# Two layers of the second block: token blocks of the output projection in another order, and four probability copies moved ahead of exponentials

## The reference, cut to what matters

```python
def hybrid_layer(x, ...):
    h = rmsnorm(x, norm_w)
    aq, ak, av, ag, bq, bk, bv, bg, cu, cg = split(h @ w_in)        # 1024 -> 4608
    o_a = diff_attention(aq, ak, av, ...) * silu(ag)    # 4 heads, two softmax maps m = 0, 1 of width 64
    o_b = retention(bq, bk, bv, ...)      * silu(bg)    # 4 heads
    o_c = multiscale_pool(cu, ...)        * silu(cg)    # 4 groups
    return x + concat([o_a, o_b, o_c]) @ w_out          # 1536 -> 1024
```

## Time and profile before

| | |
|---|---|
| median of 3 runs | 2766.0 us (2764.51 to 2766.5) |
| the profiled execution | 2769.01 us, span 2767.2 us, mean granted TensorE clock 0.992 |
| TensorE busy | 2710.3 us (98% of the span) |
| VectorE busy | 1857.4 us (67%) |
| ScalarE busy | 1323.2 us (48%) |
| GpSimd busy | 140.4 us (5%) |
| chain that ended last | PE 84%, DVE 8%, ACT 4%, DMA 1%, the rest about 1% each or less |

### The profile page before, as it was taken

One profiled execution on the slowest core, in us unless ns is written; L12 is line 12 of the kernel. 1 busy time (PEld: TensorE's weight loads), 2 busy tenths in 40 slices (PEclk: granted clock), 3 DMA queues, 4 the chain that ended last, 5 costly groups with the idle time before them and its releaser, 6 DMA issues.

```text
span 2767.2 us, 44384 instructions
## 1 busy us (share of the span) xinstructions
PE 2710.3 (98%) x17512; PEld 1740.6 (63%) x17512; DVE 1857.4 (67%) x2793; ACT 1323.2 (48%) x2116; POOL 140.4 (5%) x119
## 2 busy tenths in 40 slices
PE   9999999999999999999999999999999999999999
PEld 6886476654688646885566654688546555465544
DVE  7994475646899539993576555999446775567754
ACT  4663365543566425662465442566333535335442
POOL 1000022100100001000022000100000002000010
PEclk9999999999999999999999999999999999999999
DMA  5443312222344332433322212444332231322312
GB/s 162 112 118 114 122 49 67 84 77 84 92 111 117 118 116 79 118 105 118 107 69 62 84 61 99 122 115 113 114 122 92 64 104 61 107 73 68 93 61 84
DMA packets 325306, 265.66 MB, mean 96 GB/s; under 512 B 25228, under 2 KB 288652, under 8 KB 324528
## 3 DMA queue, kind: packets, MB, share of 16 engines
q1 hardware_dynamic: 322608, 254.57, 29.8%
q10 hardware_dynamic: 1952, 7.05, 1.0%
q0 software_dynamic: 608, 2.11, 0.2%
HBM read 257.40 MB, written 4.21 MB: 95 GB/s over the span
## 4 chain that ended last, share of the span: by engine, by line
PE 84%; DVE 8%; ACT 4%; DMA 1%; DVEq 1%; issue 1%; SPq 0%; ACTq 0%; POOL 0%
PE pu L471 12%; PE pu L472 12%; PE pu L473 12%; PE pu L598 6%; PE pu L597 6%; PE pu L599 6%; PE pm L471 5%; PE pm L472 5%; PE pm L473 5%; PE pm L597 2%; PE pm L598 2%; PE pm L599 2%; PE pm L896 2%; DVE w_lo L1089 2%; PE pm L669 2%; PE pm L883 1%
## 5 line engine op out<-in xcount | busy, mean ns | idle before, releaser
L1089 DVE SCALAR_TENSOR_TENSOR w_lo<-stage,w_hi 128x2048 f16<-128x2048 f32 (+1 forms) x156 | 356.8, 2287 | 399.0 <-ACT w_hi L1818 394.8
L1818 ACT ACTIVATE w_hi<-stage 128x2048 f16<-128x2048 f32 (+1 forms) x147 | 273.3, 1859 | 498.2 <-PE pm L473 376.2
L471 PE MATMUL pu<-h_hi,w_hi 128*128 128x512 f16 x912 | 348.3, 382 | 5.9 <-DVE w_lo L1089 5.9
L472 PE MATMUL pu<-h_lo,w_hi 128*128 128x512 f16 x912 | 347.6, 381 | 0.0
L473 PE MATMUL pu<-h_hi,w_lo 128*128 128x512 f16 x912 | 347.3, 381 | 0.0
L471 PE MATMUL pu<-w_hi,arena 128*128 128x512 f16 x512 | 196.2, 383 | 6.5 <-ACT arena L2131 6.5
L472 PE MATMUL pu<-w_lo,arena 128*128 128x512 f16 x512 | 196.3, 383 | 0.0
L473 PE MATMUL pu<-w_hi,arena 128*128 128x512 f16 x512 | 195.9, 383 | 0.0
L471 PE MATMUL pm<-w_hi,arena 128*128 128x512 f16 x512 | 194.0, 379 | 0.0
L472 PE MATMUL pm<-w_lo,arena 128*128 128x512 f16 x512 | 194.0, 379 | 0.0
L473 PE MATMUL pm<-w_hi,arena 128*128 128x512 f16 x512 | 194.0, 379 | 0.0
(11 more groups left out here) (330 smaller groups left out, 6225.4 us busy)
## 6 DMA issues: line engine op xcount, KB each, us to landing
stage<-in_w_in_dram SPq DMA_DIRECT2D x136, 512.0 KB, 4.5
stage<-in_w_ffn_gate_dram SPq DMA_DIRECT2D x88, 512.0 KB, 3.9
stage<-in_w_ffn_up_dram SPq DMA_DIRECT2D x88, 512.0 KB, 5.1
stage<-in_w_ffn_down_dram SPq DMA_DIRECT2D x80, 512.0 KB, 4.0
stage<-in_w_out_dram SPq DMA_DIRECT2D x40, 512.0 KB, 4.2
stage<-in_w_in_dram SPq DMA_DIRECT2D x24, 256.0 KB, 3.3
stage<-in_w_ffn_down_dram SPq DMA_DIRECT2D x16, 256.0 KB, 4.2
stage<-in_w_branch_hgrn_dram SPq DMA_DIRECT2D x8, 512.0 KB, 3.5
```

Of the source, the lines that this page charges most:

```text
L471: nc.tensor.matmul(ps, w1, r_hi, start=first, stop=False)
L472: nc.tensor.matmul(ps, w1, r_lo, start=False, stop=False)
L1089: V.scalar_tensor_tensor(out=w_lo[:, s, 0:n], in0=stage[:, s, 0:n], scalar=WSCALE, in1=w_hi[:, s, 0:n], op0=ALU.mult, op1=ALU.subtract).th ...
L1818: A.activation(w_hi[:, s, 0:n], stage[:, s, 0:n], ACT.Copy, scale=WSCALE).then_inc(hi_split, 1)
```

## The change: what it does

In the tensor engine's list: (a) `scores2` has its waits ahead of the one matmul whose bank they guard, rather than ahead of both; in slots 8 and 12 map 1 goes first. (b) The first pass of the output projection takes token blocks 0 and 1 through all four chunks, after the Silus up to ("cg", 0), and then blocks 2 and 3, after the last Silu. In ScalarE's list: (c) in slots 8 and 12 the copy of the transposed probabilities stands ahead of the exponentials; before and elsewhere it stands behind them. In VectorE's list: (d) the retention heads and pool groups wait for the Silu of the values that they use, not for the last one owed.

```diff
@@ tensor: scores2
-                if i >= 2:
-                    pe.wait_ge(pt_ready, t.at("pt_ready", i - 1))
-                if i % 4 == 2 and i > 2:
-                    pe.wait_ge(o_sq, t.now("o_sq"))
-                if i in (8, 12):
-                    pe.wait_ge(o_cp, t.next("o_cp"))
-                if i % 4 == 3 and i > 3:
-                    pe.wait_ge(o_rt, t.next("o_rt"))
                 hd, b = divmod(i, NB)
-                for m in range(2):
+                for m in (1, 0) if i in (8, 12) else (0, 1):
+                    if m == 0 and i >= 2:
+                        pe.wait_ge(pt_ready, t.at("pt_ready", i - 1))
+                    if m == 1 and i % 4 == 2 and i > 2:
+                        pe.wait_ge(o_sq, t.now("o_sq"))
+                    if m == 1 and i in (8, 12):
+                        pe.wait_ge(o_cp, t.next("o_cp"))
+                    if m == 1 and i % 4 == 3 and i > 3:
+                        pe.wait_ge(o_rt, t.next("o_rt"))
@@ tensor: mixer2, first pass of the output projection
-                        pe.wait_ge(evac_a, t.now("evac_a"))
-                    for n, (at, k) in enumerate(slot_ks[i % 3]):
...
+                        for unit in range(2):
+                            pe.wait_ge(evac_a, t.now("evac_a") - 1 + unit)
+                            for n, (at, k) in enumerate(slot_ks[0]):
+                                pe.wait_ge(m_ready, t.now("m_ready") + n + 1)
+                                for b in (2 * unit, 2 * unit + 1):
+                                    last = token_part(pu[b], b, 0, [(at, k)], acc, k == 0, False)
@@ vector: mixer2_slot, retention heads
-                    settle()
+                    v.wait_ge(evac_a, t.at("evac_a", evacuated(MIX2_ORDER.index(("bg", (hd - 1) // 2)) + 1, True, MIX2_ORDER)))
@@ vector: pool_post
-                    settle()
+                    v.wait_ge(evac_a, t.at("evac_a", evacuated(MIX2_ORDER.index(("cg", gr // 2)) + 1, True, MIX2_ORDER)))
@@ vector: mixer2, after pool_post()
+                settle()
@@ scalar: mixer2_slot; taken(i) is the wait for pt_done and the copy to AT that stood in the slot
+                if q in (8, 12):
+                    taken(q - 1)
                 if q < 16:
                     ...   (wait for mx_ready, two exponentials)
...
-                if 1 <= q <= 16:
...
+                if 1 <= q <= 16 and q not in (8, 12):
+                    taken(q - 1)
```

More of the change, by code:

```diff
@@ L1007, in mixer2 @@
                         pe.wait_ge(evac, t.now("evac") + 2)
-                        pe.wait_ge(evac_a, t.now("evac_a"))
-                    for n, (at, k) in enumerate(slot_ks[i % 3]):
[L1010 to L1013, removed]
+                        for unit in range(2):
[4 more added lines that the diff above has]
+                                    last = token_part(pu[b], b, 0, [(at, k)], acc, k == 0, False)
+                    else:
+                        for n, (at, k) in enumerate(slot_ks[i % 3]):
+                            if i < 3:
+                                pe.wait_ge(m_ready, t.now("m_ready") + 4 * i + n + 1)
+                            for b in range(NB):
+                                last = token_part((pu if i < 3 else pm)[b], b, i % 2, [(at, k)], acc, k == 0, k == OUT2_LATE[-1])
                     last.then_inc(unit_done, 1)
@@ L2085, in copy_scale, with taken @@
                 A.activation(r_post[:], ps[:], ACT.Copy).then_inc(o_cp, 1)
+            def taken(i):
+                s_.wait_ge(pt_done, t.next("pt_done"))
+                b = i % NB
+                A.activation(AT[:, :, b * P:(b + 1) * P], pm[2 * (i % 2)][:].rearrange("p (k c) -> p k c", k=NB), ACT.Copy).then_inc(pt_ready, 1)
             def mixer2_slot(q):
```

## The result

The changed kernel takes 2745.34 us (median of 4 runs, 2744.75 to 2745.9), the kernel before 2766.25 (4 runs). The ratio is 0.9925, with a 95% interval of 0.9913 to 0.9938: 20.9 us less. In a later comparison it was 2743.88 (5 runs) against 2766.51 (9 runs), ratio 0.9923 (0.9909 to 0.9936).

A forecast was written before the change was run, and what follows sets the result against it. The prediction took TensorE, busy for 98% of the span, as the bound. Its terms, 7.4 + 6.7 + 7.4 + 0 = 21.5 us off the 2766.0 median, gave 2744.5 us, with a range of 2740 to 2752.

The forecast's parts named there:

- (c), 7.4 us: Scores of slots 9 and 13, both layers: moving the probability copy up removes four stalls, 3 x 1.78 + 2.05 us.
- next meeting point: Scores of slot 10, where TensorE next needs ScalarE's copies: ScalarE is in time, so none of the gain is given back.
- slack that was put at 0.38 us: Before slot 10's scores: ScalarE's copies end at 2195.29, the scores want to start at 2195.67, leaving 0.38 us.
- (b), 6.7 us: Output projection's start, once per layer: splitting the first pass removes the whole 3.35 us stall for the last Silu.
- The clock, 7.4 us: TensorE's slow clock behind stalls: 1.64 us in slot 9, 2.58 and 3.15 in first projection passes, all taken as won.
- The rival in which it doesn't come back: Projection: the clock falls anyway at the pool products, so only 14.1 us are gained, 2752; chance 0.10.
- (a), 0: Score pairs of slots 7, 11 and 15: moving the wait gains 0 us, as the later matmul still waits.
- the wait isn't won back: Rival at scores of slots 7, 11 and 15: moving the wait gains another 2.3 us, 2742; chance 0.08.
- no pair comes apart: Rivals denied: score pairs come apart where a wait stands between (2761 us, chance 0.03) or in every slot (2778, 0.02).
- (d), 0: VectorE's last retention head starts some 4 us earlier, but half a projection pass hides it anyway: 0 us.
- More falls in the timed runs: Rival at slots 9 and 13: all four stalls lose 1.64 us, not one, so 4.9 more gained, 2739.6; chance 0.07.

The follow-up runs named there:

- only_b: Kernel before the change with only the output projection's first pass split into two halves: 2755.06 us, ratio 0.9958.
- no_d: Changed kernel without VectorE's waits for the Silu of the values it uses: 2745.69 us, ratio 0.9929 to the kernel before.
- filler: Kernel before the change with 28 spare matmuls in TensorE's wait at the start of the output projection, the wait kept: 2761.91 us, ratio 0.9985.
- one_half: Changed kernel with both score matmuls of a pair on the same rows of the array: 2770.64 us, ratio 1.0019 to the kernel before.
- only_a: Kernel before the change with only the score waits moved next to the matmul they guard: 2764.88 us, ratio 0.9998.
- only_c: Kernel before the change with only the probability copy moved ahead of the exponentials in slots 8 and 12: 2757.3 us, ratio 0.9969.
- before: The kernel without any of the changes: 2766.25 us, median of 4 runs.
- only_d: Kernel before the change with only VectorE waiting for the Silu of the values it uses: 2764.99 us, ratio 0.9995.
- pool_late: Changed kernel with slot 28's last pool product behind the first half of the projection's first pass: 2742.37 us, ratio 0.9915 to the kernel before; again 2742.64.

## Why the prediction was right, step by step

- **(c), 7.4 us:** 7.4 measured, with the next meeting point as worked out. The slack that was put at 0.38 us is 0.21. ScalarE came up a little less than worked out: its high half starts 7.96 us after the scores of slot 8 (8.40 before, so 0.44 instead of 0.49), and its squares 15.21 after them, where the working gives 15.04. The step holds, with less to spare than it said.
- **(b), 6.7 us:** 6.9. The lone score matmul with its 1.05 us was the nearest row, but the pool product is followed after 0.96. Half a pass hides the last Silu (`only_b`), also without (d) (`no_d`).
- **The clock, 7.4 us:** 6.8. The fall in slot 9 was right at 1.6. The first passes were over-counted by 0.26 us each: I compared them with 10.36, the distance between two high halves, but from the first product to the first high half it's 10.62 at full clock. That the clock is lowered by the standing still, assumed in the prediction, is shown by `filler` and `only_b`. The rival in which it doesn't come back is out.
- **(a), 0:** 0.6. The reason was right, `one_half` shows the pair's concurrency by itself. The size was a little off: the successor comes 1.42 us after the first of the two, 0.10 a place sooner than the wait and the pair one after the other. (By starts the wait costs 0.46 us, 8.05 less 7.59, where the view lists 0.39 of idle time.) The rivals are out: the wait isn't won back, and no pair comes apart.
- **(d), 0:** 0.3 beside the other parts, by the tails of `no_d` and the changed kernel, and not told from none in the medians. The reason given holds for the projection, where half a pass hides VectorE's head. What it missed lies elsewhere: a low weight half that came late, and VectorE's pause in slot 7 of the second layer.
- **More falls in the timed runs:** the prediction called the four stalls of part (c) alike and put the one fall down to the phase. They weren't alike: the one with the fall was the longest, 2.05 us against 1.78 by its own figures, and the same one shows it in all four profiles that have VectorE's pause as well as the stall. The other three show none in any profile. The projection's two starts show a fall in all four kernels that keep the stall without a filler (`before`, `only_a`, `only_c`, `only_d`). There the stall is 3.27 us each time, but the first passes take from 11.95 to 13.51 us, so what the slow clock costs does vary. The Trainium skill ("TensorE: Matmul & The Clock Gate", "Part 1: The HAM clock gate") says that the point at which the clock changes depends on the phase in which the work meets the gate; these differing lengths agree with it.

The errors (+0.2, -0.6, +0.6) nearly cancelled, so 2744.5 against 2745.34 is closer than the terms. Some of that is luck. The terms come from one profile with a mean clock of 0.992, while the timed runs of the same kernel beside the experiments had 0.994 to 0.996. In four profiles the two first passes together took 5.2, 4.0, 3.0 and 5.3 us more than twice 10.62, 4.4 on average. By that an average run would gain 0.8 us less than this profile: an estimate, which would account for most of the way from the tail's 22.0 us to the medians' 20.9.

What stays open: why VectorE pauses without (d), and whether the length of a stall alone decides over the fall of the clock.

## What to carry to other kernels

When one engine is busy nearly all the time, list its few waits, and for each ask three things: what the waiting instruction was queued behind, which engine is late at the next meeting point once the wait is gone, and whether the clock fell after it. Here the slow clock behind the stalls was a third of the gain, and spare matmuls alone won most of that third without removing a stall. Moving a wait from a pair of concurrent matmuls to one of them wins next to nothing, since the pair ends with its later member.

## What the runs showed that I had not expected

The same instructions ahead of the change take different times. The first score pair of the second block starts at 2119.6, 2118.1 and 2115.8 us in the profiles of the kernel before and two of the changed one, and as early as 2115.3 in `only_c`; the program of the first block is the same in all. Much of this is slow clock in some executions and not in others. From 484 to 499 us the granted clock is 0.89 in the two late ones and 1.00 in the two early ones, and the late ones lose 1.6 us to the others there. From 1662 to 1676 and from there to 1690 it's 0.91 and 0.96 in the kernel before and 1.00 in the other three, which costs it 1.5 us. From the first score pair on, two profiles of the changed kernel agree to 0.1 us over 626 us (625.64, 625.70), and the two of `pool_late` at 623.78. So a difference below some 4 us between the spans of two executions needs a look at where it arises: in the tail even the 0.6 us of (a) can be read, in the medians it can't.
